# A Mamba-2, mLSTM and differential-attention stack on one core: the cell gate computed feature by feature, decay rows spread over four heads' columns

## What is computed

```python
z_a, xbc, dt_raw, z_b, q, k, v, ig, fg, og = split(h @ ab_w_in)
y_a = _ssd(xbc, dt_raw, z_a, ...)                 # 16 heads of 64
y_b = _mlstm(q, k, v, ig, fg, og, z_b, ...)       # 4 heads of 256
x = x + concat([y_a, y_b]) @ ab_w_out
# in _ssd, per chunk
decay = where(causal, exp(a_cs[l] - a_cs[s]), 0)
y_diag = (C B^T * decay) @ xdt;  y_off = (C @ state) * exp(a_cs)
state = state * exp(a_cs[-1]) + B^T @ (exp(a_cs[-1] - a_cs) * xdt)
y = y_diag + y_off + xs * d_skip
return _rms(y * silu(z_a)) * norm_g               # rms over groups of 512
# in _mlstm, per chunk
s = (q k^T) * exp(d_log - m_t)                    # d_log: causal log decays
num = s @ v + w_inter * (q @ c_mem);  h = num / max(|den|, exp(-m_t))
c_mem = dec * c_mem + (g * k)^T @ v
h = _rms(h * sigmoid(o_raw)) * norm_g             # rms per head of 256
return h * silu(z_b)
```

## Time and profile before

| | before |
|---|---|
| three runs | 1575.18, 1576.92, 1577.39 us (median 1576.92) |
| profiled execution, its time | 1573.38 us |
| profiled execution, its span | 1571.6 us, mean granted TensorE clock 0.992 |
| busy | PE 1525.6, DVE 907.6, ACT 649.0, POOL 566.1 us |
| start, projection | 0 to 17.3 us, 17.3 to 559.0 us |
| scan with its middle products | 559.0 to about 762 us |
| layer 2 | to 1571.6 us |

### The profile page before, as it was taken

The page is one execution under the profiler, slowest core; times in us unless marked ns, Lnnn a source line. Parts: engine busy times, 40 slices in busy tenths (PEclk is TensorE's granted clock), DMA queues, the critical chain, the costliest instruction groups (busy, mean ns, idle before and its releaser), DMA issues.

```text
span 1571.6 us, 23657 instructions
## 1 busy us (share of the span) xinstructions
PE 1525.6 (97%) x9114; PEld 1314.0 (84%) x9114; DVE 907.6 (58%) x1484; ACT 649.0 (41%) x1272; POOL 566.1 (36%) x325
## 2 busy tenths in 40 slices
PE   8999999999999999999999999999999999999897
PEld 7798989898999987877788877888888888787686
DVE  7675878684843469999344272345544245554623
ACT  6542534353532233444345252345555333556321
POOL 3245454545344346567565330132212013211110
PEclk9999999999999999999999999999999999999899
DMA  5133333333334345765675330122111112113612
GB/s 178 41 122 94 122 94 121 94 121 94 121 108 135 100 160 186 227 199 175 220 267 201 121 94 14 28 61 76 53 54 34 34 28 80 54 35 114 254 67 107
DMA packets 151085, 176.43 MB, mean 112 GB/s; under 512 B 9671, under 2 KB 126659, under 8 KB 149955
## 3 DMA queue, kind: packets, MB, share of 16 engines
q1 hardware_dynamic: 150810, 174.92, 34.2%
q10 hardware_dynamic: 168, 0.06, 0.0%
HBM read 122.46 MB, written 52.43 MB: 111 GB/s over the span
## 4 chain that ended last, share of the span: by engine, by line
PE 47%; DVE 1%; ACT 1%; issue 1%; DMA 1%; POOL 0%; SPq 0%; POOLq 0%; ACTq 0%; DVEq 0%
PE b_ps L2404 22%; PE b_ps L2449 4%; PE b_ps L2424 4%; PE b_ps L2354 3%; PE b_ps L2356 3%; PE b_ps L2355 3%; PE b_ps L2436 2%; PE b_ps L2506 2%; PE b_ps L2507 2%; PE b_ps L2508 2%; PE b_ps L2457 1%; PE b_ps L2372 0%; DMA b_yy<-z 0%; DMA z<-b_y_T 0%; ACT a_aT L2056 0%
## 5 line engine op out<-in xcount | busy, mean ns | idle before, releaser
L1925 POOL TENSOR_TENSOR b_w<-b_w_raw,b_w 128x1024 fp32r<-128x1024 f32 x66 | 158.4, 2400 | 357.5 <-DVE b_w L2184 253.6
L2404 PE MATMUL b_ps<-a_h_hi,b_w 128*128 128x512 f32 x768 | 265.7, 406 | 2.9 <-DVE a_h_lo L2162 2.9
L393 POOL TENSOR_TENSOR b_w<-b_y_T,b_w 128x1024 fp32r<-128x1024 f32 x54 | 141.1, 2615 | 189.7 <-ACT b_w L451 189.7
L2404 PEld LDWEIGHTS b_ps<-a_h_hi,b_w 128*128 128x128 f32 x768 | 145.0, 189 | 37.1 <-issue 3.9
L2404 PE MATMUL b_ps<-a_h_lo,b_w 128*128 128x512 f32 x384 | 150.6, 392 | 0.0
L941 PE MATMUL b_ps<-b_w,p_hi 128*128 128x256 f32 x768 | 139.2, 283 | 0.0
L700 DVE SCALAR_TENSOR_TENSOR b_w_raw<-p_out_raw,p_cols,b_w_raw 128x1024 f32<-128x1024 f32 x60 | 119.8, 2003 | 12.8 <-ACT b_w_raw L482 11.4
L941 PEld LDWEIGHTS b_ps<-b_w,p_hi 128*128 128x128 f32 x768 | 120.1, 192 | 0.6
L941 PE MATMUL b_ps<-b_w,p_lo 128*128 128x256 f32 x384 | 108.7, 283 | 0.0
L2195 DVE CUSTOM_DVE_ANT_0 b_y_T<-b_ps,a_neg_dist 128x128 f32<-128x128 f32 (+5 forms) x96 | 72.1, 777 | 63.3 <-PE b_ps L2424 52.7
L451 ACT CAST b_w<-b_y_T 128x1024 fp32r<-128x1024 f32 x60 | 62.7, 1045 | 106.5 <-DVE b_y_T L661 55.0
(11 more groups left out here) (417 smaller groups left out, 3616.6 us busy)
## 6 DMA issues: line engine op xcount, KB each, us to landing
b_y_T<-in_ab_w_in SPq DMA_DIRECT2D x33, 512.0 KB, 4.3
tok<-p_out_raw SPq DMA_DIRECT2D x64, 256.0 KB, 2.3
b_w_raw<-in_ab_w_out SPq DMA_DIRECT2D x32, 512.0 KB, 3.7
b_w_raw<-in_c_w_in SPq DMA_DIRECT2D x32, 512.0 KB, 4.1
feat<-b_w_raw SPq DMA_DIRECT2D x20, 512.0 KB, 2.7
c_fe<-feat SPq DMA_DIRECT2D x7, 1280.0 KB, 6.6
yt<-b_y_T SPq DMA_DIRECT2D x8, 1024.0 KB, 10.9
b_y_raw<-yt SPq DMA_DIRECT2D x32, 256.0 KB, 3.9
```

Of the source, the lines that this page charges most:

```text
L393: gp.tensor_tensor(w_lo[s % SLOTS][:, :, :], operand(n, split_of(n, p))[:, :, :], w_hi[s % SLOTS][:, :, :].bitcast(F32), ALU.subtract).the ...
L1925: gp.tensor_tensor(w_lo[:, w, :], w_raw[u % W_RAW][:, :], w_hi[:, w, :].bitcast(F32), ALU.subtract).then_inc(S["l_wlo"], 1)
L2404: mm = pe.matmul(o, x, y, start=(k == 0 and q == 0), stop=(k == KT - 1 and q == 2))
```

## The change

1. **Constants.** The host arranges gains, taps and the skip vector as one array of 128x140, loaded by one DMA straight into columns. The row DMAs, the transposes L1008, L1201, L1203 and their VectorE copies go.
2. **Cell gate turned.** The two z_b blocks are made with weights stationary and 512 tokens moving, as feature blocks are, go through silu, then through a second ScalarE operation that multiplies by the cells' norm gain (`gains_of_quarter`, 8 of 128x512 per block), and are stored feature by feature to `zt0`. In the scan the gate is multiplied where y is turned (`turn` part 0 takes `gate_cells` in place of the gain columns), so VectorE's L1628 goes; the scaling by the rms is four ScalarE operations of 128x256 (`memory_norm`). A fourth DMA per chunk loads the gate cells; semaphore counts go from 32 to 48.
3. **Spread rows.** The decay rows and the mLSTM rows are kept as 128x512 with each head's row nonzero only in its own quarter of the columns (`dec_bd`, `ml_bd`; type fp32r). One selecting product of 512 columns takes the place of four of 128.
4. **Order in the scan.** e_end goes from VectorE to GpSimd, GpSimd's power for the cells goes ahead of its addition L1479, the tables go ahead of `cmem` on VectorE, qs, c_dec, st and gk go ahead of wt's first half, TensorE starts decays 0 and 1 after the first and the second `cmem` update, `num` runs over heads 2, 3, 0, 1, and ScalarE does all of wm before the SSD squares.
5. **Ends.** Chunk 0 has no products with the zero state and memory (num has 4 in place of 8, no yoff, no wint) and copies in place of updates. Chunk 7 makes no memory or state update; `mid_products` follows `ydiag` directly. Two of the four low weight units there are made by VectorE, and two of y's low parts are made earlier on VectorE.
6. In each block after the first, VectorE's sum T4 comes before the second turn and the quarters of U2, with the counts `G_FREE`, `G_NEEDS` adapted.

```diff
@@ decay_rows
-    for k in range(4):
-        h = 4 * q + k
-        pe.matmul(ps[:, bank, k * P:(k + 1) * P], keep["head_sel"][:, h:h + 1].broadcast_to([P, P]),
-                  keep["dec_rows"][:, par * P:(par + 1) * P], start=(k == 0), stop=False, skip_group_check=True)
+    pe.matmul(ps[:, bank, :], keep["head_sel"][:, q:q + 1].broadcast_to([P, P]), keep["dec_bd"][:, par, :],
+              start=True, stop=False, skip_group_check=True)
@@ scan, tensor: weights
-                    pe.wait_ge(S["d_cmem"], n * 4)
+                    pe.wait_ge(S["d_cmem"], n * 4 - 3)
                     decays(n, par, 0)
+                    pe.wait_ge(S["d_cmem"], n * 4 - 2)
                     decays(n, par, 1)
...
-                for k in range(4):
-                    mm = pe.matmul(ps[:, 7, k * P:(k + 1) * P], row_of(1, k), keep["ml_rows"][:, :], start=True, stop=True)
-                mm.then_inc(S["p_wint"], 1)
+                if behind_first(n):
+                    pe.wait_ge(S["d_cmem"], n * 4)
+                    pe.matmul(ps[:, 7, :], rows_of(1), ml_bd, start=True, stop=True).then_inc(S["p_wint"], 1)
+                pe.matmul(ps[:, 6, :], rows_of(0), ml_bd, start=True, stop=False, skip_group_check=True)
@@ scan, tensor: outputs
-                pe.wait_ge(S["a_dec"], n * 4 + 4)
-                for h in range(ML_HEADS):
+                for h in (2, 3, 0, 1):
+                    if h < 2:
+                        pe.wait_ge(S["a_dec"], n * 4 + 3 + h)
...
+                if is_last(n):
+                    return
...
-            pe.wait_ge(S["d_cmem"], 4 * TILES)
+            pe.wait_ge(S["d_h"], 4 * TILES)
@@ projection, tensor
-                    if kinds[n] == "f":
+                    if kinds[n] == "f" or gate_turned(n):
@@ projection, scalar: after each step k of a block
+                    if kinds[n] == "t" and k == 2:
+                        gains_of_quarter(n, 0, 0)
+                    if after(n, "t") and k < 3:
+                        gains_of_quarter(n - 1, *((1, 1), (1, 0), (0, 1))[k])
@@ scan, scalar
+            def memory_norm(n):
+                act.wait_ge(S["l_rstdm"], n + 1)
+                for h in range(ML_HEADS):
+                    yb = y[:, D + h * ML_V:D + (h + 1) * ML_V]
+                    a = nc.scalar.activation(yb, yb, ACT.Copy, scale=rms[:, 2 + h:3 + h])
+                a.then_inc(S["a_yb"], 1)
...
             def body(n, par, prior):
                 memory_squares(n)
-                decays(n + 1, (0, 1))
+                memory_norm(n)
+                decays(n + 1, (0, 1, 2))
+                memory_weights(n + 1)
                 ssd_squares(n)
-                decays(n + 1, (2,))
-                memory_weights(n + 1)
                 decays(n + 1, (3,))
@@ scan, gpsimd
-                gp.wait_ge(S["d_eend"], n + 1)
+                    gp.tensor_tensor(e_end[:, :], dec[:, :, P - 1:P].rearrange("p h a -> p (h a)"),
+                                     g[:, T_EACS:T_EACS + SSD_HEADS], ALU.mult).then_inc(S["l_eend"], 1)
@@ scan, vector: outputs
-                dve.wait_ge(S["l_rstdm"], n + 1)
-                for h in range(ML_HEADS):
-                    v = slice(h * ML_V, (h + 1) * ML_V)
-                    yb = y[:, D + h * ML_V:D + (h + 1) * ML_V]
-                    a = dve.scalar_tensor_tensor(out=yb, in0=yb, scalar=rms[:, 2 + h:3 + h], in1=gates(n, par, 1)[:, v],
-                                                 op0=ALU.mult, op1=ALU.mult)
-                a.then_inc(S["d_yb"], 1)
@@ scan, vector: turn
-                    dve.tensor_tensor(y_T[par][:, 4 * b:4 * b + 4, :], b4(i),
-                                      last(gcols[:, 4 * b:4 * b + 4], P), ALU.mult).then_inc(S["d_yT"], 1)
+                    by = last(gcols[:, 4 * b:4 * b + 4], P) if part else gate_cells(n, par)[:, 4 * b - 8:4 * b - 4, :]
+                    dve.tensor_tensor(y_T[par][:, 4 * b:4 * b + 4, :], b4(i), by, ALU.mult).then_inc(S["d_yT"], 1)
@@ scan, sync
-                sp.wait_ge(S["d_yb"], n + 1)
                 sp.wait_ge(S["l_yz"], n + 1)
                 load_chunk(sp, chunk, feat, tok, n + 2, par)
                 if behind_first(n):
                     store_y(n - 1, 1 - par)
+                sp.wait_ge(S["d_yT"], n * 4 + 2)
+                load_gate_cells(sp, chunk, n + 2, cell_gate[par], in_landed[par])
```

389 lines of the change are left out of this document (221 added, 168 removed).

## The result

The changed kernel takes 1556.37 us, median of four runs (1553.52 to 1560.14); the kernel before, run beside it, 1576.63. The ratio is 0.9874, with its 95% interval 0.9854 to 0.9894. 1555 was forecast, with the range 1547 to 1566. The number is right.

What follows compares the result with a forecast made beforehand. TensorE bounds the projection; a loop through TensorE and VectorE sets the scan period. Savings 3.8 + 0.9 + 0.4 + 2.7 + 10.2 + 3.8 = 21.8 us off 1576.92 give 1555, range 1547 to 1566.

Steps and rivals of the forecast that it cites:

- The loop: Scan period between memory updates: first leg 8.05 for 10.33, second 12.3, period 20.3 for 22.07; saves 10.2 us over six.
- The stall of den: Scan's second leg: VectorE's tiny den operations meet GpSimd's xe, stalling up to 1.7 us, 0.8 reaching the memory products.
- The z_b blocks: Projection: two blocks go from 40.31 us as token blocks to 38.43 as feature blocks, saving 3.8 us.
- The other sum there: By the Trainium skill's isolated figures the two z_b blocks would save 0.4 us together, making the total 18.4.
- The start: Kernel's start: the transposes' wait for the last row DMA goes; saves 0.9 us, between 0 and 2.07.
- term of 0.4 for the last block's decays: Decays in the projection's last block: 2 x 0.2, saving 0.4 us.
- The first chunk: Scan's chunk 0: less work shortens the path to the first memory update by 2.7 us, between 1 and 3.9.
- the third rival: TensorE's clock falls to 1.2 GHz around chunk 0 and stays for chunks; 1594 us for two; chance 0.03.
- The last chunk: Scan's chunk 7: unneeded work and a shorter first leg, less waits for the turn; net 3.8 us, between 1 and 8.
- No stall: Scan: den misses xe or the stall is absorbed; period is TensorE's floor, 19.7 us; total 1549; chance 0.2.
- The new wait in the first leg: Scan's first leg: ScalarE's longer row makes `st` wait for wm, leg stays 10 us; total 1565; chance 0.17.
- Plain fp32: Scan's products of 512 do not run as fp32r: 32 us more in eight chunks, total 1587; chance 0.01.

Runs made afterwards that it cites:

- at equal addresses: The two z_b blocks computed by tokens again, against the changed kernel with x's tiles at 128 modulo 256; one execution, 1558.38 us.
- the first profile: The profiled execution of the changed kernel from its first measurement, nothing altered; 1558.86 us.
- the unread products: Twelve bf16 products of 512 that nobody reads, added to TensorE's waits in chunk 0 of the changed kernel; 1554.24 us, ratio 0.9876.
- the second profile: Profiled execution from repeating the changed kernel unaltered; that repeat's median was 1557.02 us, ratio 0.9887.
- the second set of runs: The changed kernel run again unaltered, beside the kernel before; 1557.02 us, median of five, ratio 0.9887.

## Why the prediction was right, point by point

- **The loop.** "TensorE leads now": right. First legs of 7.87 in the mean against 8.05, and `st` waits for qk. Put back one at a time, the scaling by the rms costs VectorE's side 1.02 us per period (first legs of 8.96) and the four products of 128 cost TensorE's 0.77 (8.63).
- **The stall of den**, "up to 1.7, of which 0.8 us arrives": shown, by taking the meeting away. The operation took 1.89 us, and the stall was worth 0.73 per period. The term was mis-sized on another side: 11.5 us "without waits" is 11.74, measured without the stall. The operation that met xe was held by 1.7 us in all six periods; in the one shown 1.20 of it arrived at the update (12.94), in the mean 0.93 (12.67). With 7.87 + 12.67 = 20.54 for 20.35 the six periods gave 8.9 us for 10.2. That "every small operation in the trace that met a GpSimd operation waited" is not so: in the trace of before the three copies of the tables ran in 0.17 to 0.19 us (647.50 to 647.85) beside GpSimd's power of 128x4 (647.21, 1.02 us), and so do those of the changed kernel (618.57). What held the first of them, in the run with the tables behind the update, was GpSimd's addition of 128x1024. The rule of the Trainium skill (page "SBUF — State Buffer", section "Who interferes with whom") agrees with the two meetings of den, whose operations have two SBUF inputs; for the table's copy, which has one, it would take the two-port mode, and no row tells the mode.
- **The z_b blocks**, 3.8 us: the mechanism was right (4.5 at equal addresses), the result was not. From the first product to the end of these blocks the profile shows 377.40 us before and 377.29 after. The step that failed is "This is measured on the same engine with the same number format, so I take it": it held the matmuls' spacing for a property of their form, and it is one of their tiles' place too. The token blocks behind them then gave 1.8 us by the same cause (164.08 us before and with the tiles placed as before, 162.30 in the changed kernel). The other sum there has a slip: 48 x 0.109 and 24 x 0.216 us, unrounded, are 0.06 apart, seven times in each of two blocks, so it comes to 0.84 us and 18.8 in place of 0.4 and 18.4; with 4.5 measured the trace stays against it.
- **The start**, 0.9: right, with the next to be late where it was expected. The term of 0.4 for the last block's decays is 0.33: from the start of the last product to that of the second mask it is 1.14 us before (558.82 to 559.96) and 0.81 after (556.01 to 556.82).
- **The first chunk**, 2.7, and 0.4 for the decays: +0.74 in the first profile, -2.87 in the second of the same kernel, and 2.9 to 4.4 less than before in six of the nine profiles without the unread products. So the term fits most executions and the first profile is one in which the clock took it back. The work is less: at full clock, with the unread products in the waits, it is 16.1 us from the last product of the projection to the first update (556.16 to 572.23), against 21.03 before, which had a short low stretch itself. In the first profile TensorE, idle for 1.4 us, then for 1.8 and once more before `num` (564.25), fell to 1.2 GHz by 564 and stayed there to 576: `ydiag`'s 32 products took 6.92 us for 3.68. It is the third rival, on the scale of a part of one chunk and not of two; it had been priced only where it decides. Why the stretch is long in some executions and short in others stays open.

```profile
567.82 6.92 PE L1337 MATMUL b_ps<-s_xdt,s_wt 128*128 128x64 f32 x32
```

- **The last chunk**, 3.8: right with 3.55, and 3.10 in the second profile. Both waits are there, 1.74 us for the turn, which was held against it, and 1.40 for h, which was not named.
- **The rivals.** "No stall" did not happen, and its 19.7 us is about what the kernel does once the meeting is taken away (19.8). The new wait in the first leg did not come: seven of the eight `st` waited for TensorE's qk, and one, for 0.6 us, for ScalarE. Plain fp32 did not come: 0.97 us of TensorE's time per period were saved. SyncE's queue delayed nothing.
- **The sum.** In the profiled execution 14.4 us came of 21.8, in the second profile 16.3; in the medians 20.3, and 18.2 in the second set of runs (1575.17 and 1557.02). The forecast was nearer to the first medians than its terms were to the traces, and part of that is luck: how long each execution was at the lower clock.
